# Odd mixer of a fused block kernel: a new order for the queues of ScalarE, VectorE and TensorE

## The chip, the cores and the metric

The kernel runs on one core of a Trainium2 chip. The metric is the device time of one execution in microseconds (us), the median of three runs. The core's engines each take their instructions from a queue of their own, in order, and wait for one another by semaphores: PE (TensorE, matmuls and transposes), DVE (VectorE), ACT (ScalarE), POOL (GpSimd) and SP, which issues the weight transfers. PEld is PE's weight load.

## What is computed

Two small transformer blocks in float32 on 256 tokens of width 1024, one after the other. The change is in the odd mixer, the Mamba-2 layer of the first block, cut here to what matters:

```
def odd_mixer(u, w_in, conv_w, conv_b, dt_bias, a_log, d_skip, out_norm_w, w_out):
    proj = (u @ w_in)
    z, xbc, dt = jnp.split(proj, [C_D_INNER, C_D_INNER + C_XBC], axis=-1)
    xbc = jax.nn.silu(causal_dwconv(xbc, conv_w) + conv_b)
    xs, b_in, c_in = jnp.split(xbc, ...)
    dt = jax.nn.softplus(dt + dt_bias)
    a = -jnp.exp(a_log) * dt
    y = ssd_chunked_scan(xs * dt[..., None], a, b_in, c_in) + d_skip[:, None] * xs
    y = y.reshape(bsz, seq, C_D_INNER) * jax.nn.silu(z)
    y = rmsnorm(y.reshape(bsz, seq, C_GROUPS, C_D_INNER // C_GROUPS), out_norm_w...)
    return (y.reshape(bsz, seq, C_D_INNER) @ w_out)
```

C_D_INNER is 2048, in four groups of 512 columns (8 heads of 64). The scan is over two blocks of 128 tokens here: what a block does within itself, and what the second gets from the state of the first.

## The kernel before

**Weights.** Every weight matrix comes from HBM in slots of 1 MB, each used as two granules of 128 x 1024. A float32 product is made of three matmuls on rounded parts, so each granule is split: ACT copies it to its high part (hi, L732, the copy is L741), DVE subtracts to get the low part (lo, L1373, L1379), PE multiplies high by high, low by high and high by low (L2182 to L2184, twelve matmuls to a granule). SPLITS = 4 granules can be held split: hi of granule g waits until PE has used granule g - 4 (gran_used), lo waits for hi, PE for lo. hi(k) and lo(k) in a queue stand for the next k granules.

**The odd mixer** (ACT L1065, DVE L1722, PE L2538) projects columns in the order OD_ORDER: B and C of the scan, dt, and then for the four groups in turn x and z. A projection is four granules into PSUM banks 0 and 1; out(k) on ACT (L1081) evicts it, and PE waits for that (proj_out) before the next projection writes these banks. B, C and the x of each group are turned to channels by PE (to_convolve, L2550), convolved (first_tap on ACT, L1091, convolve on DVE, L1732), put through Silu (conv_silu, L1100), and turned back (to_tokens, L2557; x_tokens, L1105, copies the result).

**The loop over g = 0, 1, 2** (ACT L1184, DVE L1831, PE L2637) does the scan of group g beside the projection of x of group g + 1 (beside_x) and of z of group g + 1 (beside_z; step k of them stands behind granule k). Its steps: c_times_b (PE L2564, copied by cb_copy, L1110); masked_decays (DVE L1751), rows (PE L2571, L2572) and exps (ACT L1123) make the decays of four heads, q = 0 to 3, in banks 4 and 5; segment (DVE L1768) multiplies them by c_times_b; weighted_x (DVE L1757 to L1759); state (PE L2578, copied by state_copy, L1115) and from_state (PE L2583) by way of bank 7; inside (PE L2595) into bank 6; skip (DVE L1773); gate (DVE L1783 to L1789) adds up and multiplies by z; squares, root, inverse_root, normed (ACT L1130, L1137, DVE L1794, ACT L1144) are the rmsnorm; turn_y (PE L2604), y_high (ACT L1151) and y_low (DVE L1801) bring the result to the two parts in which it goes into the last product. The work of group 3 stands behind the loop, beside the granules of w_out (down, L2233). All of this order is written out by hand, one list per engine.

## Time and profile before

| | us |
|---|---|
| median of 3 runs | 2990.28 (2987.95 to 2993.25) |
| the profiled execution | 2991.3 |
| its span | 2989.5 |
| PE, DVE, ACT busy in the span | 2772.0, 2100.8, 1682.2 |
| the loop, g = 0, 1, 2 (from the first matmul of its x projection to that of the next) | 47.4, 51.8, 44.9 to its last inside |
| from there to the last turn_last | 58.9 |

The page of the profile gives busy times by engine, the chain of work that ended last, and groups of instructions by source line. The trace gives single instructions with their start, their length and what ended the idle time before them, and sums over any stretch. PEclk, the clock that TensorE was granted, is a share of 2.4 GHz: 0.50 is 1.2 GHz. A row of windows gives the stretch and its length, then busy time and instructions of PE, PEld, DVE, ACT and POOL, PEclk, the DMA share and GB/s.

### The profile page before, as it was taken

The numbers are of one execution on the slowest core, as the hardware profiler recorded it, in microseconds if no ns is written. First come the engines' busy times: TensorE is split into PE (matmuls) and PEld (weight loads), VectorE is DVE, ScalarE is ACT, GpSimd is POOL, SyncE is SP. The second block draws the span as 40 slices with busy tenths as digits, with TensorE's granted clock in tenths as the row PEclk, the third lists the DMA queues.
The fourth block names the chain that finished last, engine by engine and source line by source line (L and its number), as shares of the span: only waits on it lengthen the run. The fifth ranks groups of instructions, "written<-read, shape, count | busy, mean of one in ns | idle before, by whom it ended". The sixth has DMA issues, their size and how long they took to land.

```text
span 2989.5 us, 35811 instructions
## 1 busy us (share of the span) xinstructions
PE 2772.0 (93%) x12921; PEld 2262.7 (76%) x12921; DVE 2100.8 (70%) x2339; ACT 1682.2 (56%) x2178; POOL 596.4 (20%) x321
## 2 busy tenths in 40 slices
PE   7999899999997799979778998799999999999997
PEld 6888778878976578868456887677878788787875
DVE  4556768778365565452458785588999888999897
ACT  4456454454275564442343443177777877778785
POOL 1000039999000000004007994000000000000000
PEclk9999999999899899989879998799999999999999
DMA  8545147778342245533017883189999999999994
GB/s 281 184 162 179 34 151 238 249 266 279 115 162 85 74 146 195 184 113 112 1 57 248 283 294 127 43 319 337 354 337 348 354 338 351 330 353 350 342 353 167
DMA packets 278012, 664.55 MB, mean 222 GB/s; under 512 B 12868, under 2 KB 21344, under 8 KB 277904
## 3 DMA queue, kind: packets, MB, share of 16 engines
q1 hardware_dynamic: 263344, 609.74, 57.7%
q0 software_dynamic: 14560, 53.36, 5.4%
q8 instruction: 70, 1.15, 0.2%
q14 instruction: 38, 0.31, 0.0%
HBM read 662.00 MB, written 1.05 MB: 222 GB/s over the span
## 4 chain that ended last, share of the span: by engine, by line
PE 79%; DVE 13%; ACT 5%; issue 2%; DMA 0%; DVEq 0%; ACTq 0%; SPq 0%
PE ps L2182 23%; PE ps L2184 23%; PE ps L2183 23%; DVE w_lo L1379 4%; ACT w_hi L741 2%; PE ps L2298 1%; PE ps L2852 1%; PE ps L2364 1%; PE ps L2766 1%; DVE xt L2054 1%; DVE small L1940 1%; PE ps L2728 1%; DVE xt L1732 1%; PE ps L2810 0%; DVE xn L1458 0%
## 5 line engine op out<-in xcount | busy, mean ns | idle before, releaser
L1379 DVE TENSOR_TENSOR w_lo<-w_raw,w_hi 128x1024 fp32r<-128x1024 f32 x1156 | 1534.9, 1352 | 522.5 <-ACT w_hi L741 496.3
L741 ACT ACTIVATE w_hi<-w_raw 128x1024 fp32r<-128x1024 f32 x1156 | 1210.3, 1058 | 835.0 <-PE ps L2184 834.2
L2182 PE MATMUL ps<-w_hi,act_hi 128*128 128x512 f32 (+1 forms) x3424 | 1353.4, 395 | 65.2 <-DVE w_lo L1379 33.5
L2184 PE MATMUL ps<-w_lo,act_hi 128*128 128x512 f32 (+1 forms) x3424 | 1327.9, 388 | 0.0
L2183 PE MATMUL ps<-w_hi,act_lo 128*128 128x512 f32 (+1 forms) x3424 | 1327.1, 388 | 0.0
L2182 PEld LDWEIGHTS ps<-w_hi,act_hi 128*128 128x128 f32 x3424 | 651.6, 190 | 213.9 <-DVE w_lo L1379 51.5
L2184 PEld LDWEIGHTS ps<-w_lo,act_hi 128*128 128x128 f32 x3424 | 650.9, 190 | 133.0
L2183 PEld LDWEIGHTS ps<-w_hi,act_lo 128*128 128x128 f32 x3424 | 652.1, 190 | 127.1 <-issue 3.5
L620 POOL TENSOR_TENSOR scr<-scr 128x1024 f32<-128x1024 f32 x98 | 287.3, 2932 | 8.2
L618 POOL TENSOR_SCALAR scr<-scr,small 128x1024 f32<-128x1024 f32 x98 | 194.7, 1987 | 6.4
L601 POOL DMA_DIRECT2D scr<-in_ada_w x48 | 36.8, 767 | 404.0 <-DVE h L1463 384.8
L872 ACT ACTIVATE act_hi<-ps 128x512 fp32r<-128x512 f32 (+1 forms) x87 | 62.7, 721 | 78.0 <-PE ps L2298 78.0
L1504 DVE TENSOR_TENSOR act_lo<-ps,act_hi 128x512 fp32r<-128x512 f32 (+1 forms) x87 | 73.9, 849 | 34.3 <-ACT act_hi L872 34.2
L2298 PEld LDWEIGHTS ps<-cst,hp 128*128 128x128 f32 x456 | 54.5, 140 | 24.5 <-DVE hp L1524 9.0
L674 POOL DMA_DIRECT2D scr<-in_ctx x1 | 0.8, 767 | 358.1 <-DVE h L1463 358.1
L2298 PE MATMUL ps<-cst,hp 128*128 128x128 f32 x456 | 64.2, 273 | 8.3 <-DVE hp L1524 6.9
L1528 DVE TENSOR_TENSOR hp<-sg,ps 128x512 f32<-128x512 f32 (+1 forms) x63 | 46.6, 740 | 33.1 <-PE ps L2184 33.1
L2273 PE MATMUL ps<-cst,xn 128*128 128x128 f32 x96 | 22.0, 424 | 42.9 <-DVE xn L1438 26.8
L1524 DVE SCALAR_TENSOR_TENSOR hp<-ps,rn,sg 128x512 f32<-128x512 f32 (+1 forms) x48 | 31.6, 700 | 36.1 <-PE ps L2184 36.1
L2273 PEld LDWEIGHTS ps<-cst,xn 128*128 128x128 f32 x96 | 19.7, 227 | 46.5 <-DVE xn L1438 21.2
L635 POOL TENSOR_TENSOR wbc<-xn,rope 128x512 f32<-128x512 f32 x2 | 2.7, 1364 | 239.8 <-ACT xn L1252 239.7
L1940 DVE TENSOR_REDUCE small<-ps 128x2 f32<-128x1024 f32 x16 | 19.6, 1224 | 35.2 <-PE ps L2766 35.2
(455 smaller groups left out, 1691.2 us busy)
## 6 DMA issues: line engine op xcount, KB each, us to landing
w_raw<-in_moe_w SPq DMA_DIRECT2D x336, 1024.0 KB, 6.9
scr<-in_ada_w POOLq DMA_DIRECT2D x48, 1024.0 KB, 5.9
w_raw<-in_ffn_w_gate SPq DMA_DIRECT2D x44, 1024.0 KB, 5.2
w_raw<-in_ffn_w_up SPq DMA_DIRECT2D x44, 1024.0 KB, 5.4
w_raw<-in_ffn_w_down SPq DMA_DIRECT2D x44, 1024.0 KB, 4.9
w_raw<-in_ff_w SPq DMA_DIRECT2D x42, 1024.0 KB, 5.9
w_raw<-in_odd_w_in SPq DMA_DIRECT2D x20, 1024.0 KB, 5.1
w_raw<-in_even_w_in SPq DMA_DIRECT2D x14, 1024.0 KB, 5.2
```

The costliest lines, as they stand in the source:

```text
L618: pool.tensor_scalar(product, w, x, 0.0, ALU.mult, ALU.add).then_inc(ada_mul, 1)
L620: pool.tensor_tensor(dst[:, cols], dst[:, cols], product, ALU.add).then_inc(ada_sum, 1)
L741: act.activation(w_hi[:, g % SPLITS, 0:c * width], w_raw[:, s % RING, o:o + c * width], ACT.Copy).then_inc(hi_done, 1)
L872: act.activation(act_hi[:, base:base + c, 0:tbs * P], src, ACT.Copy).then_inc(hhi_done, 1)
L1379: dve.tensor_tensor(w_lo[:, g % SPLITS, 0:c * width], w_raw[:, s % RING, o:o + c * width], w_hi[:, g % SPLITS, 0:c * width].bitcast(F32), ...
L1504: dve.tensor_tensor(act_lo[:, base:base + c, 0:tbs * P], src, act_hi[:, base:base + c, 0:tbs * P].bitcast(F32), ALU.subtract).then_inc(hlo ...
L1528: dve.tensor_tensor(view[0], view[1], ps[:, 6:6 + tbs, 0:width], ALU.mult).then_inc(hid_done, 1)
L1940: link(dve.tensor_reduce(m, ps[:, 2 * (u % 2):2 * (u % 2) + 2, :], AX_X, ALU.max))
L2182: pe.matmul(out_ap, hi, whi, start=start, stop=False)
L2183: pe.matmul(out_ap, lo, whi, start=False, stop=False)
L2184: return pe.matmul(out_ap, hi, wlo, start=False, stop=stop)
L2298: ins = pe.transpose(banks(6, tbs)[:, o:o + P], hp[:, tb * BANK + k * P:tb * BANK + k * P + P], ident)
```

## The change

Steps of the odd mixer's queues are put in another order on ACT, DVE and PE. Nothing is computed otherwise.

- hi and lo stand one granule at a time between the other steps, where they stood in twos; three granules of the next projection are split at the start of a turn of the loop, where it was four.
- out(5 + 2g) stands ahead of state_copy and of one more hi; out(6 + 2g) stands behind the first half of the Silu alone (conv_silu becomes two silu_half, and the second half moves into the next turn).
- gate(g, 1), squares(g, .) and root of a group move into the next turn. The product with the state that gate(g, 1) began with is a step of its own, from_before, with a semaphore of its own, og_or.
- On PE c_times_b stands behind granule 0 of x, both rows(0), rows(1) and to_tokens behind granule 1, state behind granule 3; both inside(g, 0), inside(g, 1) and to_convolve behind granule 0 of z. turn_y goes to banks 4 and 5, where it was 2 and 3.
- Behind the loop half_down does the first three granules of w_out for 128 tokens at a time, so that they can start before banks 2 and 3 are free.

On ACT, in turn 1 of the loop, from x_tokens (scr<-ps 128x2x512) to out (xn<-ps,rn). Before:

```order
L1105 ACTIVATE scr<-ps 128x2x512
L1110 ACTIVATE xt<-ps 128x256
L1144 ACTIVATE scr<-scr,rstd 128x512 x2
L1123 ACT_TABLE_LOAD
L1123 ACTIVATE hp<-ps,dtw 128x128 x4
L741 ACTIVATE w_hi<-w_raw 128x1024 x2
L1123 ACTIVATE hp<-ps,dtw 128x128 x4
L1115 ACTIVATE scr<-ps 128x512
L741 ACTIVATE w_hi<-w_raw 128x1024 x2
L1081 ACTIVATE xn<-ps,rn 128x512 x2
```

After (line numbers are up by 1 to 5; scr,ssq is squares, rt is root):

```order
L742 ACTIVATE w_hi<-w_raw 128x1024
L1115 ACTIVATE xt<-ps 128x256
L1135 ACTIVATE scr,ssq<-scr 128x512
L1142 ACT_TABLE_LOAD
L1142 ACTIVATE rt<-ssq,epsc 128x2
L742 ACTIVATE w_hi<-w_raw 128x1024
L1110 ACTIVATE scr<-ps 128x2x512
L1128 ACT_TABLE_LOAD
L1128 ACTIVATE hp<-ps,dtw 128x128 x8
L742 ACTIVATE w_hi<-w_raw 128x1024
L1149 ACTIVATE scr<-scr,rstd 128x512 x2
L1082 ACTIVATE xn<-ps,rn 128x512 x2
```

The eviction now stands behind two w_hi rather than four, and ahead of the copy of the state (scr<-ps 128x512); what was squares and root of the turn before stands here.

On DVE, from the end of turn 0 to the low part behind weighted_x (the three scr<-scr,dtw). Before:

```order
L1379 TENSOR_TENSOR w_lo<-w_raw,w_hi 128x1024
L1751 TENSOR_TENSOR sg<-cst,dtw 128x512 x2
L1794 RECIPROCAL rstd<-rt 128x2
L1379 TENSOR_TENSOR w_lo<-w_raw,w_hi 128x1024
L1757 TENSOR_TENSOR scr<-scr,dtw 128x512
L1758 TENSOR_TENSOR scr<-scr,dtw 128x512
L1759 TENSOR_TENSOR scr<-scr,dtw 128x512
L1379 TENSOR_TENSOR w_lo<-w_raw,w_hi 128x1024
```

After (line numbers are up by 19 to 21; the first three rows are what is left of gate(0, 1)):

```order
L1806 TENSOR_TENSOR scr<-scr,ps 128x512
L1809 TENSOR_TENSOR scr<-scr,xt 128x512
L1810 TENSOR_TENSOR scr<-scr 128x512
L1398 TENSOR_TENSOR w_lo<-w_raw,w_hi 128x1024
L1770 TENSOR_TENSOR sg<-cst,dtw 128x512 x2
L1398 TENSOR_TENSOR w_lo<-w_raw,w_hi 128x1024
L1815 RECIPROCAL rstd<-rt 128x2
L1398 TENSOR_TENSOR w_lo<-w_raw,w_hi 128x1024
L1776 TENSOR_TENSOR scr<-scr,dtw 128x512
L1777 TENSOR_TENSOR scr<-scr,dtw 128x512
L1778 TENSOR_TENSOR scr<-scr,dtw 128x512
L1398 TENSOR_TENSOR w_lo<-w_raw,w_hi 128x1024
```

Three w_lo stand between gate and weighted_x, one on each side of the decays (sg) and one behind the reciprocal, where one stood ahead of the decays and one behind the reciprocal.

On ACT, at the end of turn 1, from first_tap to the squares. Before:

```order
L1091 ACTIVATE xt<-ps,colv 128x256 x4
L741 ACTIVATE w_hi<-w_raw 128x1024
L1123 ACTIVATE hp<-ps,dtw 128x128 x4
L741 ACTIVATE w_hi<-w_raw 128x1024
L1100 ACT_TABLE_LOAD
L1100 ACTIVATE xt<-xt 128x512 x2
L741 ACTIVATE w_hi<-w_raw 128x1024 x2
L1081 ACTIVATE scr<-ps,rn 128x512 x2
L1130 ACTIVATE scr,ssq<-scr 128x512 x2
```

After:

```order
L1092 ACTIVATE xt<-ps,colv 128x256 x4
L742 ACTIVATE w_hi<-w_raw 128x1024
L1128 ACTIVATE hp<-ps,dtw 128x128 x4
L742 ACTIVATE w_hi<-w_raw 128x1024
L1128 ACTIVATE hp<-ps,dtw 128x128 x4
L1100 ACT_TABLE_LOAD
L1100 ACTIVATE xt<-xt 128x512
L1082 ACTIVATE scr<-ps,rn 128x512 x2
L1100 ACTIVATE xt<-xt 128x512
```

Between the last exps and the eviction of z (scr<-ps,rn) one half of the Silu is left; two w_hi and the other half are gone from there.

The diff, cut to what the working speaks of (ACT, DVE, PE):

```diff
-                hi(2)
+                hi(1)
                 first_tap(2)
                 hi(2)
+                silu_half(2, 0)
                 out(4)
-                conv_silu(2)
-                act.wait_ge(sv_in, n(sv_in))
-                act.activation(dtw[:, T_ECUM, :], dtw[:, T_CUM, :], ACT.Exp)
-                act.activation(dtw[:, T_EDEC, :], dtw[:, T_REST, :], ACT.Exp).then_inc(sv_out, 1)

                 for g in range(3):
+                    silu_half(2 + g, 1)
+                    hi(1)
+                    if g:
+                        squares(g - 1, 0)
+                    hi(1)
+                    cb_copy()
+                    if g:
+                        squares(g - 1, 1)
+                        root(2 * g - 2, 2)
+                    else:
+                        act.wait_ge(sv_in, n(sv_in))
+                        act.activation(dtw[:, T_ECUM, :], dtw[:, T_CUM, :], ACT.Exp)
+                        act.activation(dtw[:, T_EDEC, :], dtw[:, T_REST, :], ACT.Exp).then_inc(sv_out, 1)
+                    hi(1)
                     x_tokens(g)
-                    cb_copy()
+                    exps(g, 0, 4)
+                    exps(g, 1, 5)
+                    hi(1)
                     if g:
                         normed(g - 1, 0)
                         normed(g - 1, 1)
-                    exps(g, 0, 4)
-                    hi(2)
-                    exps(g, 1, 5)
+                    out(5 + 2 * g)
+                    hi(1)
                     state_copy()
-                    hi(2)
-                    out(5 + 2 * g)
                     if g:
-                        y_high(g - 1, 0, 2)
-                        y_high(g - 1, 1, 3)
-                    exps(g, 2, 4)
+                        y_high(g - 1, 0, 4)
+                        y_high(g - 1, 1, 5)
+                    hi(1)
                     first_tap(3 + g)
                     hi(1)
+                    exps(g, 2, 4)
+                    hi(1)
                     exps(g, 3, 5)
-                    hi(1)
-                    conv_silu(3 + g)
-                    hi(2)
+                    silu_half(3 + g, 0)
                     out(6 + 2 * g)
-                    squares(g, 0)
-                    squares(g, 1)
-                    root(2 * g, 2)
-
+
...
+                def from_before(g):
+
+                    dve.wait_ge(og_off, n(og_off))
+                    dve.tensor_tensor(eight(o_off), eight(ps[:, 7, :]), bc(of(T_ECUM, 1, g), C_DIM), ALU.mult).then_inc(og_or, 1)
+
...
+                        dve.wait_ge(og_or, g + 1)
                         link(dve.tensor_tensor(x, x, o_off, ALU.add))
...
                 for g in range(3):
+                    if g:
+                        gate(g - 1, 1)
+                    lo(1)
                     masked_decays(g, 0)
                     masked_decays(g, 1)
+                    lo(1)
+                    if g:
+                        inverse_root(2 * g - 2, 2)
+                    lo(1)
                     if g == 0:
                         dve.wait_ge(sv_out, n(sv_out))
-                    else:
-                        inverse_root(2 * g - 2, 2)
-                    lo(1)
                     weighted_x(g)
                     lo(1)
                     segment(0)
+                    segment(1)
                     masked_decays(g, 2)
-                    lo(1)
-                    segment(1)
                     masked_decays(g, 3)
                     skip(g, 0)
                     lo(1)
+                    if g:
+                        y_low(g - 1, 0, 4)
+                        y_low(g - 1, 1, 5)
                     gate(g, 0)
-                    if g:
-                        y_low(g - 1, 0, 2)
-                        y_low(g - 1, 1, 3)
-                    segment(2)
                     lo(1)
                     convolve(3 + g, 0)
-                    segment(3)
                     lo(1)
-                    convolve(3 + g, 1)
+                    from_before(g)
+                    segment(2)
                     skip(g, 1)
                     lo(1)
-                    gate(g, 1)
-                    lo(1)
-
+                    segment(3)
+                    convolve(3 + g, 1)
+
+                gate(2, 1)
+                lo(1)
                 masked_decays(3, 0)
                 masked_decays(3, 1)
+                segment(0)
+                segment(1)
+                masked_decays(3, 2)
+                masked_decays(3, 3)
+                weighted_x(3)
                 inverse_root(4, 2)
...
+                def half_down(chunks, tb, skip=0):
+
+                    for k, chunk in enumerate(chunks):
+                        g = gp[0] + skip + k
+                        pe.wait_ge(lo_done, g + 1)
+                        for nh in range(2):
+                            ins = three(ps[:, 2 * tb + nh, :], chunk, slice(tb * P, tb * P + P), g, nh * BANK, BANK,
+                                        skip + k == 0, False)
+                        if tb:
+                            ins.then_inc(gran_used, 1)
...
                     def beside_x(k):
                         if k == 0:
+                            if g:
+                                pe.wait_ge(og_or, g)
+                            c_times_b(g)
+                        if k == 1:
+                            if g:
+                                pe.wait_ge(og_e, 4 * g)
+                            rows(0, 4)
+                            rows(1, 5)
                             pe.wait_ge(cv_act, CV + 2 * (3 + g))
                             to_tokens(2 + g, 2)
-                        if k == 1:
-                            rows(0, 4)
+                        if k == 3:
+                            state(g)
                             if g:
-                                pe.wait_ge(og_yz, 2 * g)
-                            c_times_b(g)
-                        if k == 2:
-                            rows(1, 5)
-                            state(g)
-                        if k == 3:
-                            inside(g, 0)
-                            if g:
+                                pe.wait_ge(og_e, 4 * g + 2)
                                 pe.wait_ge(og_n, 2 * g)
-                                pe.wait_ge(o_tc, 2 + g)
-                                turn_y(g - 1, 0, 2)
-                                turn_y(g - 1, 1, 3)
+                                turn_y(g - 1, 0, 4)
+                                turn_y(g - 1, 1, 5)
...
                     def beside_z(k):
                         if k == 0:
+                            inside(g, 0)
                             inside(g, 1)
+                            pe.wait_ge(o_tc, 2 + g)
+                            to_convolve(3 + g)
+                        if k == 1:
                             pe.wait_ge(og_e, 4 * g + 1)
+                            if g:
+                                pe.wait_ge(og_lo, 2 * g - 1)
                             rows(2, 4)
-                        if k == 1:
+                            from_state(g)
+                        if k == 2:
                             pe.wait_ge(og_e, 4 * g + 2)
-                            rows(3, 5)
-                            from_state(g)
-                            pe.wait_ge(o_tc, 2 + g)
                             if g:
                                 pe.wait_ge(og_lo, 2 * g)
-                            to_convolve(3 + g)
-                        if k == 2:
+                            rows(3, 5)
+                        if k == 3:
                             inside(g, 2)
-                        if k == 3:
                             inside(g, 3)
...
+                pe.wait_ge(og_or, 3)
+                c_times_b(3)
+                pe.wait_ge(og_e, 12)
+                rows(0, 4)
+                rows(1, 5)
+                pe.wait_ge(proj_out, 8 + 11)
+                pe.wait_ge(og_lo, 4)
+                half_down((o_slot(0), o_slot(1)), 0)
                 pe.wait_ge(cv_act, CV + 12)
                 to_tokens(5, 2)
-                pe.wait_ge(og_yz, 6)
...
+                half_down((o_slot(2),), 0, 2)
                 pe.wait_ge(o_tc, 5)
-                down((o_slot(0),), True)
-                pe.wait_ge(og_n, 6)
-                turn_y(2, 0, 5)
+                half_down((o_slot(0), o_slot(1), o_slot(2)), 1)
+                gp[0] += 3
                 state(3)
-                down((o_slot(1),))
+                down((o_slot(3),))
                 inside(3, 0)
...
                 inside(3, 1)
                 pe.wait_ge(og_e, 14)
+                pe.wait_ge(og_n, 6)
+                turn_y(2, 0, 4)
+                turn_y(2, 1, 5)
+                down((o_slot(4),))
+                from_state(3)
+                down((o_slot(5),))
+                pe.wait_ge(og_lo, 6)
                 rows(2, 4)
-                from_state(3)
-                down((o_slot(4), o_slot(5)))
+                rows(3, 5)
+                down((o_slot(6),))
                 inside(3, 2)
```

## Rows read from the trace of the kernel before

**Rows 1.** The page: the chain that ended last, shares by engine.

```profile
PE 79%; DVE 13%; ACT 5%; issue 2%; DMA 0%; DVEq 0%; ACTq 0%; SPq 0%
```

**Rows 2.** Windows: turns 1 and 2, the tail behind the loop, turn 0.

```profile
937.50:989.30 51.80, 39.92 (x172) 30.24 (x172) 28.26 (x45) 27.70 (x52) 0.00 (x0) 0.86 0.23 82
989.30:1034.20 44.90, 39.32 (x172) 29.82 (x172) 22.75 (x35) 24.00 (x46) 0.00 (x0) 0.91 0.20 71
1034.20:1093.10 58.90, 49.67 (x224) 38.52 (x224) 37.30 (x55) 36.55 (x64) 0.00 (x0) 0.91 0.35 112
890.10:937.50 47.40, 37.21 (x164) 28.39 (x164) 26.57 (x45) 23.64 (x44) 0.00 (x0) 0.90 0.27 89
```

**Rows 3.** Waits in turn 1: who for whom, us in total, times, longest.

```profile
DVE w_lo L1379 <- ACT w_hi L741: 19.2, 4, 11.3
...
PE ps L2182 <- ACT scr L1081: 6.3, 1, 6.3
...
PE ps L2578 <- DVE scr L1759: 4.4, 1, 4.4
```

**Rows 4.** Windows behind two waits of PE in turn 2.

```profile
989.00:994.50 5.50, 5.18 (x13) 4.02 (x14) 4.60 (x8) 3.18 (x7) 0.00 (x0) 0.53 0.16 26
...
1008.00:1011.00 3.00, 2.93 (x5) 1.71 (x6) 2.35 (x4) 0.82 (x2) 0.00 (x0) 0.50 0.16 35
```

**Rows 5.** Timeline of ACT, turn 1: start, length, instruction [idle before it <-releaser].

```profile
943.98 1.03 ACT L1105 ACTIVATE scr<-ps 128x1024 f32<-128x1024 f32 x1 [2.21 <-PE ps L2557]
...
948.53 1.32 ACT L1144 ACTIVATE scr<-scr,rstd 128x512 f32<-128x512 f32 x2
949.87 1.28 ACT L1123 ACT_TABLE_LOAD   x1
951.17 1.14 ACT L1123 ACTIVATE hp<-ps,dtw 128x128 f32<-128x128 f32 x4
...
985.60 0.63 ACT L1100 ACTIVATE xt<-xt 128x512 f32<-128x512 f32 x1 [3.70 <-DVE xt L1732]
986.13 1.99 ACT L741 ACTIVATE w_hi<-w_raw 128x1024 fp32r<-128x1024 f32 x2
988.02 1.24 ACT L1081 ACTIVATE scr<-ps,rn 128x512 f32<-128x512 f32 x2
```

**Rows 6.** Timeline of DVE, turn 1.

```profile
953.29 1.23 DVE L1379 TENSOR_TENSOR w_lo<-w_raw,w_hi 128x1024 fp32r<-128x1024 f32 x1 [11.33 <-ACT w_hi L741]
...
955.76 0.68 DVE L1759 TENSOR_TENSOR scr<-scr,dtw 128x512 f32<-128x512 f32 x1
...
982.89 2.67 DVE L1732 SCALAR_TENSOR_TENSOR xt<-ps,colv,xt 128x255 f32<-128x255 f32 x6
...
989.06 0.69 DVE L1786 TENSOR_TENSOR scr<-scr,ps 128x512 f32<-128x512 f32 x1
```

**Rows 7.** Timeline of PE, turn 1, at the full clock.

```profile
971.92 0.39 PE L2571 MATMUL ps<-negr,identr 128*128 128x512 f32 x1
...
973.01 1.02 PE L2583 MATMUL ps<-scr 128*128 128x512 f32 x2
973.86 1.04 PE L2550 MATMUL ps<-cst,xn 128*128 128x128 f32 x8
974.66 0.47 PE L2182 MATMUL ps<-w_hi,act_hi 128*128 128x512 f32 x1
...
977.50 1.00 PE L2595 MATMUL ps<-scr,hp 128*128 128x64 f32 x8
978.31 0.48 PE L2182 MATMUL ps<-w_hi,act_hi 128*128 128x512 f32 x1
```

**Rows 8.** Timeline of PE: waits ahead of turn 0 and behind turn 2.

```profile
890.08 0.79 PE L2182 MATMUL ps<-w_hi,act_hi 128*128 128x512 f32 x1 [4.01 <-ACT scr L1081]
...
1037.75 1.22 PE L2557 MATMUL ps<-cst,xt 128*128 128x128 f32 x8 [3.28 <-ACT xt L1100]
1042.73 1.22 PE L2564 MATMUL ps<-scr 128*128 128x128 f32 x4 [3.76 <-DVE scr L1789]
```

82 lines of the change are left out of this document (35 added, 47 removed).

## The prediction

> **What bounds the kernel now.** Look first at the chain that ended last: 79% of it lies on PE [rows 1]. So nearly everywhere only PE's own work counts, and another engine matters where PE waits. The next view, busy time by window, shows that the odd mixer is such a place [rows 2]: PE is busy 39.9 us of the 51.8 us of turn 1, while DVE is busy 28.3 and ACT 27.7. No engine is full, so the turn is as long as a chain that runs from engine to engine. From the first matmul of turn 0 to the last turn_last the odd mixer takes 47.4 + 51.8 + 44.9 + 58.9 = 203.0 us [rows 2].
>
> The waits of turn 1 say where PE stands still [rows 3]: 6.3 us for an eviction on ACT, 4.4 us for weighted_x on DVE. The timeline of ACT shows the first: behind the second half of the convolution come Silu at 985.60, two w_hi from 986.13, and only at 988.02 the eviction of z, though PE has stood since 983 [rows 3, 5]. The timeline of DVE shows the second: it stands 11.3 us at a low part (953.29) whose high part is queued on ACT behind x_tokens and the exps; weighted_x, which needs no weights, sits behind it until 955.76 + 0.7, and state on PE waits for it [rows 6]. The third cost follows from the two: behind each long wait the granted clock is 0.50 to 0.53 for 5.5 us and 3.0 us [rows 4], that is the lower level of 1.2 GHz.
>
> **What PE must do in a turn.** In rows at the full clock one granule takes 977.50 - 974.66 = 2.84 us, a call of rows 973.01 - 971.92 = 1.09, from_state 0.85 (state the same), eight transposes 974.66 - 973.86 = 0.80, inside 978.31 - 977.50 = 0.81 [rows 7]. A turn has 8 granules (22.7), 4 rows (4.4), 4 inside (3.2), state and from_state (1.7), three sets of eight transposes (2.4), c_times_b (four short ones, 0.4): 34.8 us. Turn 1 takes 51.8, so 17 us are waits and low clock.
>
> **The new order, walked through for one turn.** Zero is the first matmul of x. Durations besides those above, as the distance to the next instruction: w_hi 0.95, an eviction 1.2, x_tokens 1.0, both normed 1.3, a table load 1.28, an exps 1.0, Silu 0.6 [rows 5]; w_lo 1.14, a convolution half 2.6, the three steps of gate 2.1 [rows 6].
>
> First half. PE: granule 0 to 2.8, c_times_b, granule 1 to 6.1, two rows to 8.3, to_tokens to 9.1, granules 2 and 3 to 14.8, state to 15.6, turn_y. ACT: Silu half, w_hi, squares, w_hi (free from 2.8), cb_copy, squares, root with its load, w_hi (free from 6.1) until 7.3; then it waits for to_tokens: x_tokens 9.1 to 10.1, load 11.4, exps twice 13.5, w_hi 14.4, normed 15.7, eviction of x 16.9. PE's turn_y waits for normed until 15.7 and ends at 16.5, so PE loses 0.1 ahead of it and 0.4 to the eviction, with a semaphore or two 0.7 in all. DVE: gate 2.2, w_lo 3.3, decays 4.6 (wanted at 6.1), two w_lo to 8.5, weighted_x 10.1 to 12.1, wanted by state at 14.8. The wait of 4.4 is gone, with 2.7 us to spare, and the low parts of x are ready 8 us early.
>
> Second half, from 17. PE: granule 19.8, two inside 21.4, to_convolve 22.2, granule 25.1, rows 26.2, from_state 27.0, granule 29.9, rows 31.0, granule 33.8, two inside 35.4. ACT: copies and y_high until 20, w_hi, first_tap 22.2 to 24, w_hi 26, exps 27.3, w_hi 30.9, exps 32.0, load 33.3, Silu half 33.9, eviction of z 35.1. PE's two inside (1.6 us) cover it. DVE: y_low 21.6, gate 23, w_lo and convolution half 26.8, w_lo, from_before and segment 29.3, skip, w_lo 32, segment 32.7 (wanted at 34.6), the other half 35.3, and gate in the next turn. The wait of 6.3 is gone: its cover is inside, which is 1.6 long against 1.2. Without a long wait the clock stays up.
>
> So a turn takes 34.8 + 0.7 = 35.5 us. Turn 0 has no turn_y (-0.8) but starts behind a wait as now, at the lower level for one granule (+2.3: 13 matmuls took 5.5 us there [rows 4], so twelve 5.1 against 2.8): 37.0. **Ahead of turn 0** one w_hi fewer stands before the eviction that PE waits 4.0 us for [rows 8]; one half of the Silu is moved ahead of it (0.6). I take 1.0 us, bounds 0 and 4.
>
> **The tail.** Before, PE waits 3.3 us for the Silu and 3.8 us for gate [rows 8], with smaller waits behind. After, its work is 12 granules in whole or halves (34.1), 4 rows (4.4), 4 inside (3.2), two products with the state (1.7), transposes 0.8 + 0.8 + 0.8, c_times_b 0.4: 46.2. The new order puts both rows ahead of the first granule, and they wait for DVE: gate(2, 1) 2.1, a w_lo 1.1, the first decays 0.6 stand before them, and c_times_b covers 0.4: a new wait of 3.5 us. Whether the clock falls after it is open: it did behind 6.3 and 4.4 us [rows 4], and I charge 2 us (bounds 0 and 4). Walked on as above, each later step has its input: 46.2 + 5.5 = 51.7.
>
> **Edits at no cost.** from_before adds no instruction, only its own place. Two stores of decays in banks 4 and 5 rather than one at a time, and turn_y there rather than in 2 and 3, add waits of PE (og_e, og_lo) that the walk finds met 1 us or more early. half_down does the same matmuls. SP's weight loads follow the low parts; the DMA engines are busy 0.20 to 0.35 of these stretches [rows 2] and would be at 0.3 to 0.4. POOL is idle here and not touched.
>
> **The sum.** After: 37.0 + 35.5 + 35.5 + 51.7 = 159.7, against 203.0: 43.3, and 1.0 ahead of turn 0: 44.3 us less. What follows the odd mixer is shifted. The profiled execution took 2991.3, 1.0 above the median, so 2947.0 for it and **2946 us** as a median.
>
> A rule that speaks against this: ACT changes its function set three times a turn in both orders, and one of these loads now stands between to_tokens and the eviction of x. In the rows a load starts 0.02 us behind the last normed and the exps starts 1.30 us after the load started [rows 5]. The Trainium skill, in "ScalarE: Activation LUTs", section "What ACT_TABLE_LOAD costs", gives the same 1283 ns for the load and adds a drain of about 1380 ns for each switch. The trace does not show that drain here, and the measurement decides.
>
> **The rivals.**
> - *The queues trail.* ACT has 7.8 us of steps between to_tokens and the end of the eviction of x, PE 7.4 us: any step that ACT starts late comes out on PE, and DVE carries 28 us in 35. For it: PE near full, DVE and ACT near 80%, tied at each granule. Against: the spare times above. Turns of 39 to 43 and a tail a little longer: 10 to 25 us of the gain are lost, 2953 to 2972.
> - *Each load also drains*, by the rule above. An extra 1.4 us per load would lie on PE's path once a turn and once in the tail: 5.6, so 2952. Against: the two rows of the load.
> - *The wait only moves.* PE would wait as long at the evictions, because the high parts ahead of them wait for PE. Against: in the walk ACT waits for PE to free a high part only right behind granules, never with an eviction due. 2984 to 2996.
> - *Starved for low parts (slower).* Only three granules are split at the start of a turn, and the fourth low part sits behind gate, which waits for the last inside of the turn before. It decides once DVE comes to it more than 8 us late, since granule 3 starts at 12.0. Then each granule waits for a w_hi and a w_lo in a row: 2.1 us times 24, and the clock falls to the lower level, 2.3 us times 24; less the 44: about 3050.
>
> **How the numbers follow.** Forecast 0.65, with its own range 2936 to 2953: 2936 is every wait and low clock above at nothing (0.7 x 3 + 2.3 + 5.5, and the bounds). Trailing queues 0.22, drains 0.03, a moved wait 0.05, starved 0.05. The range of 2935 to 2967 holds the first and the third and most of the second, 0.8 in all. A measurement of this kernel can tell about 0.2%, 6 us, from no change. Faster by more: 0.65 + 0.22 + 0.03 + 0.02 of the moved wait; the same: 0.02; slower: 0.05 and 0.01.
>
> **What would show it.** In the profile after: turns of 35 to 36 us; the two waits of 6.3 and 4.4 gone from PE's list, PEclk near 1.00 in turns 1 and 2; DVE's waits for w_hi no longer than 2 to 3 us; a PE wait of about 3.5 us for the decays at the start of the tail. I am wrong if ACT's Silu waits long for the convolution at a turn's start, if PE waits at state, or if low parts are late for granule 3.

## The result

| kernel | median us | runs | lowest, highest | ratio to before, 95% interval |
|---|---|---|---|---|
| before | 2989.11 | 4 | 2987.43, 2993.25 | |
| changed | 2950.3 | 4 | 2948.82, 2951.35 | 0.9875 [0.9861, 0.9889] |

The change saves 38.8 us by the medians, 1.3%; the ratio in the table, which is not the quotient of the two medians, says 1.25%, with an interval of 1.1 to 1.4%. The profiled execution of the changed kernel took 2948.8 us (span 2946.9), that of the kernel before 2991.3 (span 2989.5): 42.5 us between the two profiles. The median before is 1.2 us lower than the one the prediction started from, because a fourth run has come in.

The page of the changed kernel, the chain that ended last (before: 79% on PE [rows 1]):

```profile
PE 81%; DVE 12%; ACT 4%; issue 2%; DMA 0%; DVEq 0%; ACTq 0%; SPq 0%
```

Windows of the changed kernel, in the same columns as [rows 2] (window, its length, busy time and count of PE, weight loads, DVE, ACT, POOL, then the granted clock, DMA share, GB/s): turn 0, turn 1, turn 2, the tail to the end of the last turn_last.

```profile
892.88:929.06 36.18, 35.68 (x164) 27.80 (x165) 26.60 (x44) 22.81 (x41) 0.00 (x0) 0.95 0.43 143
929.06:964.73 35.67, 35.15 (x175) 27.54 (x174) 28.19 (x45) 27.77 (x51) 0.00 (x0) 1.00 0.34 119
964.73:1000.42 35.69, 35.16 (x174) 27.54 (x174) 28.19 (x45) 27.78 (x51) 0.00 (x0) 1.00 0.35 118
1000.42:1052.41 51.99, 48.36 (x223) 37.64 (x222) 31.74 (x46) 32.70 (x60) 0.00 (x0) 0.93 0.34 106
```

Turn 1 went from 51.8 to 35.7 us, turn 2 from 44.9 to 35.7, turn 0 from 47.4 to 36.2, the tail from 58.9 to 52.0. The four sum to 159.5, against 203.0. In turn 1 DVE and ACT are busy 28 us, as before, but in a turn that is 16 us shorter. The clock is at 1.00 (2.4 GHz) through turns 1 and 2, where it was 0.86 and 0.91.

Waits in turn 1 (who for whom: us in total, times, longest), against [rows 3]. The list has no line of PE for an eviction or for weighted_x any more, and DVE's 19.2 us behind high parts are 4.5:

```profile
ACT w_hi L742 <- PE ps L2208: 4.8, 4, 2.5
DVE w_lo L1398 <- ACT w_hi L742: 4.5, 3, 2.4
```

In the first line ACT waits for PE to free the slot of a high part; before the change that line stood at 2.0 us. It is the healthy direction, since PE is the engine that is to be full.

The timeline of PE in the changed kernel shows the waits that are left: one ahead of turn 0, one of half a microsecond in turn 0 and in turns 1 and 2 (turn 1's is shown), one at the start of the tail.

```profile
892.88 0.50 PE L2206 MATMUL ps<-w_hi,act_hi 128*128 128x512 f32 x1 [3.59 <-ACT scr L1082]
...
910.55 0.50 PE L2206 MATMUL ps<-w_hi,act_hi 128*128 128x512 f32 x1 [0.50 <-ACT xn L1082]
...
945.16 1.07 PE L2628 MATMUL ps<-cst,scr 128*128 128x128 f32 x8 [0.52 <-ACT scr L1149]
...
1004.72 0.76 PE L2595 MATMUL ps<-negr,identr 128*128 128x512 f32 x1 [3.63 <-DVE sg L1770]
```

Windows of PE alone (busy, clock, DMA share, GB/s) around the wait of the tail: up to its end, the 5.5 us behind it, and the time after.

```profile
1000.40:1004.70 4.30, 0.69 (x6) 0.78 0.00 0
1004.70:1010.20 5.50, 5.49 (x10) 0.55 0.61 191
1010.20:1023.80 13.60, 13.60 (x72) 1.00 0.11 29
```

**A measure that the clock elsewhere does not blur.** For comparing the experiments the span is split at two instructions which all kernels have: the first transposes of four in the odd mixer, to_tokens(0) (873.24 before, 876.47 after), and the last turn_last (1092.48 before, 1052.02 after). Between the two lies all that the change touches; it is called the stretch below. It is 219.2 us before and 175.6 after: 43.7 less. PE executes the same instructions in the part ahead of it in every kernel here, and so it does in the part behind.

### The profile page after: what moved, and what is told of

The parts are those of the page before. It is cut to its first block, busy times and chain, and to the rows that moved or that the text cites. A ratio compares the mean times of both kernels' runs of the same rounds, so it can differ in the third digit from the quotient of the medians.

```text
span 2946.9 us, 35814 instructions
## 1 busy us (share of the span) xinstructions
PE 2758.8 (94%) x12921; PEld 2256.2 (77%) x12921; DVE 2085.5 (71%) x2339; ACT 1680.7 (57%) x2177; POOL 590.6 (20%) x321
## 4 chain that ended last, share of the span: by engine, by line
PE 81%; DVE 12%; ACT 4%; issue 2%; DMA 0%; DVEq 0%; ACTq 0%; SPq 0%
PE ps L2206 24%; PE ps L2208 24%; PE ps L2207 24%; DVE w_lo L1398 4%; ACT w_hi L742 2%; PE ps L2322 1%; PE ps L2388 1%; PE ps L2892 1%; PE ps L2806 1%; DVE xt L2078 1%; DVE small L1964 1%; PE ps L2768 1%; PE ps L2596 0%; DVE xn L1477 0%; PE ps L2850 0%
## 5 line engine op out<-in xcount | busy, mean ns | idle before, releaser
L1964 DVE TENSOR_REDUCE small<-ps 128x2 f32<-128x1024 f32 x16 | 19.6, 1224 | 35.9 <-PE ps L2806 35.9
```

What stands on the lines that cost most here:

```text
L1964: link(dve.tensor_reduce(m, ps[:, 2 * (u % 2):2 * (u % 2) + 2, :], AX_X, ALU.max))
```

## The experiments

Each of the twelve kernels was profiled and timed, two of them twice. The twelve share one kernel before, which was timed again with each set, so each ratio is to runs of its own set. All profiles, split in the three parts (us):

| kernel | part ahead | stretch | part behind | ratio to before, 95% interval |
|---|---|---|---|---|
| before | 873.2 | 219.2 | 1897.0 | |
| changed | 876.5 | 175.6 | 1894.9 | 0.9875 [0.9861, 0.9889] |
| changed_again | 874.0 | 175.6 | 1894.8 | 0.9872 [0.9856, 0.9887] |
| loop_alone | 873.9 | 176.5 | 1893.7 | 0.9871 [0.9854, 0.9887] |
| loop_alone_again | 873.0 | 176.3 | 1894.3 | 0.9863 [0.9846, 0.9880] |
| z_evicted_late | 873.8 | 186.0 | 1897.7 | 0.9890 [0.9874, 0.9907] |
| high_parts_late | 868.3 | 188.6 | 1895.3 | 0.9897 [0.9879, 0.9914] |
| decays_first | 876.7 | 170.0 | 1893.4 | 0.9849 [0.9832, 0.9865] |
| head | 868.6 | 173.0 | 1897.3 | 0.9840 [0.9825, 0.9855] |
| head_and_decays | 874.6 | 168.0 | 1896.9 | 0.9830 [0.9816, 0.9843] |
| head_decays_too | 876.4 | 165.7 | 1892.1 | 0.9818 [0.9805, 0.9832] |
| eviction_alone | 874.8 | 211.7 | 1894.4 | 0.9975 [0.9962, 0.9989] |
| high_part_early_alone | 872.8 | 204.5 | 1893.1 | 0.9953 [0.9936, 0.9969] |
| both_places | 879.3 | 198.1 | 1897.9 | 0.9915 [0.9899, 0.9931] |

The theory of the prediction: two waits of a turn set its length, one for the eviction of z that stands behind high parts on ACT, one for weighted_x that stands behind a late high part on DVE; the rest is steps that are off PE's path once moved. Rival one: only one of the two counts, the other is covered. Rival two: the tail's gain comes from the lead of the queues, not from the tail's own order.

### Undoing one thing in the changed kernel

**z_evicted_late**

```diff
                 for g in range(3):
-                    silu_half(2 + g, 1)
-                    hi(1)
+                    if not g:
+                        silu_half(2, 1)
+                        hi(1)
...
                     silu_half(3 + g, 0)
+                    silu_half(3 + g, 1)
+                    hi(1)
                     out(6 + 2 * g)
```

> The changed kernel with one thing put back: ScalarE's second half of the Silu of Z and a w_hi (about 3.1 us) stand ahead of the eviction of Z again, on which the next turn's matmuls wait. If the eviction's place is what took the 6.3 us wait away, each turn has a wait of 2 to 3.5 us on TensorE for the eviction, turns of 38 to 39 us, and if the clock falls behind it 39 to 40: 8 to 13 us more in all (2958 to 2963). If the order of the high parts carries the gain instead, the wait stays under 1 us and the time within 2 us of 2950.

Measured: the stretch is 10.5 us longer (186.0). PE's wait for the eviction is back in turns 0 and 1, 2.83 us each, and the clock falls behind it:

```profile
929.38 0.79 PE L2207 MATMUL ps<-w_hi,act_hi 128*128 128x512 f32 x1 [2.83 <-ACT scr L1082]
```

```profile
929.30:933.30 4.00, 3.92 (x9) 3.14 (x10) 1.83 (x3) 0.64 (x3) 0.00 (x0) 0.50 0.54 161
```

Nine matmuls in 4.0 us, where at full clock 17 or 18 fit (below): here a wait of 2.8 costs 5 us in all. The stretch lies in the expected 8 to 13 us, though by two waits and not three: at the end of turn 2 the eviction is covered by the wait of 3.6 us that the tail has anyway, and turn 1 is 41.3 us, more than the 39 to 40 expected. The medians say less. 2955.1 is 4.8 above the changed kernel, under the expected range, and the intervals overlap; beside loop_alone, which was timed in the same set (2947.2), it is 7.9, where the stretches differ by 9.5.

**high_parts_late**

```diff
-                    hi(1)
                     cb_copy()
...
-                    hi(1)
                     x_tokens(g)
                     exps(g, 0, 4)
+                    hi(2)
                     exps(g, 1, 5)
```

> The changed kernel with the other thing put back: the two high parts of Z stand as a pair behind x_tokens and the first exps on ScalarE, as before the change. If VectorE's wait for a high part (11.3 us before the change, 2.4 in the changed kernel) is what held back weighted x, VectorE waits 4 to 6 us for w_hi in each turn, TensorE's state waits 2 to 4 us for weighted x, and each turn is 38 to 41 us: 8 to 15 us more (2958 to 2965). If only the eviction counts, the turns stay at 35.5 to 36.5 and the time within 2 us of 2950.

Measured: the stretch is 13.1 us longer (188.6). In turn 1 the wait list of this kernel has DVE at 9.0 us for one high part, and PE at 3.4 us for weighted_x:

```profile
DVE w_lo L1397 <- ACT w_hi L742: 10.4, 2, 9.0
ACT w_hi L742 <- PE ps L2207: 6.9, 3, 3.1
...
PE ps L2601 <- DVE scr L1777: 3.4, 1, 3.4
```

```profile
940.50:944.50 4.00, 3.99 (x11) 2.77 (x12) 4.00 (x6) 3.43 (x7) 0.00 (x0) 0.50 0.56 228
```

This is the chain that the prediction read out of the kernel before, made again by two moved lines: high part late, low part late, weighted_x late, state late, clock down (the window above starts at state). DVE's wait is 9.0, not the 4 to 6 that was expected, because x_tokens, behind which the high parts stand, waits 3.19 us for to_tokens on PE itself; the table load and the exps follow, and the w_hi comes only at 935.00, without a wait of its own:

```profile
931.65 1.03 ACT L1110 ACTIVATE scr<-ps 128x1024 f32<-128x1024 f32 x1 [3.19 <-PE ps L2580]
...
935.00 2.02 ACT L742 ACTIVATE w_hi<-w_raw 128x1024 fp32r<-128x1024 f32 x2
```

Here too the medians say less than the stretch: 2955.6 is 5.3 above the changed kernel and 8.4 above loop_alone of the same set. The rival in which only the eviction counts is out, and z_evicted_late rules out its opposite; both rest on the stretch, in which the waits themselves can be seen.

**loop_alone**, and the same kernel again as **loop_alone_again**

The loop is the changed kernel's; the steps of ACT, DVE and PE behind it are those of before (the product of from_before(3) stands right ahead of gate(3, 1), whose first step it was; half_down is gone). The start of it on DVE:

```diff
                 masked_decays(3, 1)
+                inverse_root(4, 2)
+                weighted_x(3)
                 segment(0)
-                segment(1)
                 masked_decays(3, 2)
+                y_low(2, 0, 5)
+                lo(2)
+                segment(1)
                 masked_decays(3, 3)
-                weighted_x(3)
-                inverse_root(4, 2)
                 skip(3, 0)
-                lo(4)
-                gate(3, 0)
```

> The loop of the changed kernel with the tail of the kernel before: granule 3's exps, weighted x and segments stand behind the loop again, and segment work is not spread over turn 2. If the saving comes from two separate places as the prediction's sum has it (loop and tail), the three turns stay at 36 to 37, 35.5 and 35.5 us, and the tail behind turn 2 (to the last granule's turn_last) is 58 to 59 us again instead of 51.6: 7 us longer than the changed kernel, about 2957. If the tail is short only because the loop leaves the queues further ahead, the tail stays at 52 to 53 and the time within 1 us of the changed kernel.

> New loop and old tail once more, beside the changed kernel on the same chip. The trace of the first run has 176.5 us for the stretch from the first transposed group to the last turn, the changed kernel 175.5: so 0 to 2 us slower than the changed kernel if the trace decides. If the tail's rearrangement were worth the 7 us that the first expectation of this kernel gave it, 7 us slower.

Measured: the three turns are 36.3, 35.7 and 35.9 us, as in the changed kernel, and the old tail is not 58 to 59 but 52.6 (to the end of its last turn_last):

```profile
998.20:1050.80 52.60, 48.30 (x222) 37.62 (x221) 32.05 (x46) 34.26 (x61) 0.00 (x0) 0.97 0.36 116
```

The stretch is 176.5 and 176.3, 0.9 and 0.8 longer than the changed kernel's. So the expectation that the tail's new order is worth 7 us fell, and the rival stands. Rows of PE in the old tail behind the new loop say why:

```profile
998.94 1.09 PE L2582 MATMUL ps<-cst,xt 128*128 128x128 f32 x8 [0.74 <-ACT xt L1100]
...
1000.51 0.71 PE L2589 MATMUL ps<-scr 128*128 128x128 f32 x4 [0.47 <-DVE scr L1809]
...
1002.24 0.50 PE L2596 MATMUL ps<-negr,identr 128*128 128x512 f32 x1 [1.02 <-DVE sg L1769]
...
1036.39 1.10 PE L2620 MATMUL ps<-scr,hp 128*128 128x64 f32 x8 [1.67 <-DVE hp L1786]
```

The waits for the Silu and for gate, 3.28 and 3.76 us before [rows 8], are 0.74 and 0.47 with the tail's own steps in the old order: in the new loop ACT and DVE are less behind when the loop ends. What the new tail does is trade these small waits (with one of 0.38 they sum to 4.3, and behind the one of 1.67 the clock is 0.65 and 0.69 in the two profiles) for one of 3.63 and 2 us of lower clock. The medians of the pair timed on one chip are 2949.3 (changed_again) and 2948.6: no difference that can be measured.

**changed_again**

No edit.

> The changed kernel itself, on the chip and beside the runs on which the next three are timed. By the first timing it is 38.8 us faster than before. If what differs between profiles outside the odd mixer is the clock's chance dips, its stretch from the first transposed group to the last turn is 175.5 us again to 0.2 us, while the whole moves by up to 4 us.

Measured: stretch 175.56, against 175.55 in the first profile; ratio 0.9872; 39.9 us between the medians. The part ahead is 2.5 us shorter than in the first profile, with the same instructions.

### Doing one thing in the kernel before

**eviction_alone**

```diff
-                    conv_silu(3 + g)
-                    hi(2)
+                    silu_half(3 + g, 0)
                     out(6 + 2 * g)
+                    silu_half(3 + g, 1)
+                    hi(2)
```

> The kernel before with one part of the change alone: the eviction of Z stands right behind the first half of the Silu and ahead of the other half and both high parts. The 6.3 us wait at the end of a turn should fall under 1 us. If the two waits of a turn are separate, turns fall from 45 to 52 us to 39 to 44: about 20 us less in all (2970). If the queues of ScalarE and VectorE trail as a whole, the wait comes back in the next turn at c_times_b, rows or state, and the saving is 3 to 10 us (2980 to 2986).

**high_part_early_alone**

```diff
                 for g in range(3):
+                    hi(1)
                     x_tokens(g)
                     cb_copy()
...
                     exps(g, 0, 4)
-                    hi(2)
+                    hi(1)
                     exps(g, 1, 5)
```

> The kernel before with the other part alone: one high part ahead of x_tokens and one behind the first exps instead of a pair there. VectorE's wait for w_hi (up to 11.3 us) falls, and weighted x comes earlier: the wait of state for it (4.4 us) falls to 0 to 2, while the wait for the eviction (6.3 us) stays or grows by what the others lose. 5 to 15 us less in all (2975 to 2985) if the two are separate; within 3 us of the kernel before if the eviction alone sets the turn.

Measured: 7.6 and 14.8 us off the stretch; by the medians 7.9 and 13.9. Earlier high parts alone bring more than the eviction alone. For eviction_alone 20 us were expected if the two waits are separate; that fell, and the other branch came (3 to 10 us, the wait comes back). In eviction_alone PE's wait of 6.3 us is gone, but part of it comes back at once as a wait for the decays, which stand behind gate on DVE; the wait for weighted_x is untouched. PE's waits between 930 and 955 us:

```profile
PE ps L2584 <- DVE scr L1765: 4.4, 1, 4.4
PE ps L2577 <- DVE sg L1757: 2.9, 1, 2.9
```

Behind this wait of 2.9 us for the decays the clock held at 1.00, both times that the kernel has it (the windows are in the last section).

In high_part_early_alone it is the other way round: the wait for weighted_x is gone from PE's list, and the one for the eviction stays at 6.3 in both turns.

**both_places**: the two edits together.

> The kernel before with both single parts at once: the eviction of Z between the two half Silus, and one high part ahead of x_tokens instead of two behind the first exps. Alone they took 7.6 and 14.8 us off the stretch from the first transposed group to the last turn. If they are independent, 22 us less than before, 2964 to 2966. If each only exposes the wait that the other removes, more than the sum: 30 to 38 us, and the rest of the change (gate, norm and y moved into the next turn) is worth little. If gate and c_times_b's wait sets the end of a turn in both, less than the sum, 15 to 20 us, and the moved steps carry the rest.

Measured: the stretch is 21.1 us shorter than before (198.1), by the medians 23.1. That is the sum of the two within 1.3 us, so they add. The three profiles differ in dips of the clock as well, of about 1.6 us each (an estimate from eleven matmuls rather than eighteen in 4 us): one in high_part_early_alone (behind a wait of 1.46 us), two in both_places (behind its waits of 2.87). With these taken out it is 24.3 against 7.6 + 16.4 = 24.0, the same finding. It is half of the 43.7. What PE still waits for between 942 and 985 us, the better part of a turn:

```profile
PE ps L2578 <- DVE sg L1758: 2.9, 1, 2.9
PE ps L2189 <- ACT xn L1081: 0.6, 1, 0.6
PE ps L2602 <- DVE hp L1775: 0.6, 1, 0.6
```

The other half (198.1 to the 176.4 of loop_alone, 21.7 us) belongs to what else the new loop moves: gate, squares and root into the next turn, the decays ahead of what waits, one granule's parts at a time, other banks. The first of these lines is the wait for the decays, which stand behind gate in its old place. Part of the 21.7 is the lead into the tail: PE still waits 3.29 and 3.02 us at the tail's start in both_places, 0.74 and 0.47 in loop_alone. Which of the moved steps is worth how much was not tried apart.

### Better than both kernels

**decays_first**

```diff
-                gate(2, 1)
-                lo(1)
                 masked_decays(3, 0)
                 masked_decays(3, 1)
+                gate(2, 1)
+                lo(1)
```

> The changed kernel with VectorE's two masked decays of granule 3 ahead of a gate and a low part, which nothing in the tail's start waits for. The wait of 3.6 us that TensorE has for the decays at the tail's start should be 0.3 to 0.8, and the granules behind it should not run at half clock (another 2 us): tail 46.5 to 47.5 instead of 51.6, the whole about 2945. If the clock does not come back with the wait, the gain is 3 us. If the gate is then late for normed and the last from_before, the wait turns up further down the tail and the time stays at 2949 to 2950.

Measured: the wait is 0.27, the clock stays at 1.00, and the tail is 45.9 us to the start of its last turn_last (the window reaches to its end). The stretch is 5.6 shorter, a little more than expected (the tail 51.6 less 45.9); the wait gives 3.4 of it and what is left, 2.2, goes to the clock. The median is 2942.0, where about 2945 was expected.

```profile
1001.70 0.47 PE L2595 MATMUL ps<-negr,identr 128*128 128x512 f32 x1 [0.27 <-DVE sg L1770]
```

```profile
1000.77:1047.03 46.26, 45.99 (x223) 36.53 (x222) 31.63 (x46) 32.62 (x60) 0.00 (x0) 1.00 0.39 119
```

**head**

```diff
                 act.activation(dtw[:, T_E, :], dtw[:, T_ABS, :], ACT.Exp, scale=-1.0).then_inc(act_link, 1)
+                act.activation(work[:, 0:32], m_alog, ACT.Exp)
                 act.wait_ge(act_link, n(act_link))
-                act.activation(dtw[:, T_LN, :], dtw[:, T_E, :], ACT.Ln, bias=1.0)
-                act.activation(work[:, 0:32], m_alog, ACT.Exp).then_inc(sv_out, 1)
+                act.activation(dtw[:, T_LN, :], dtw[:, T_E, :], ACT.Ln, bias=1.0).then_inc(sv_out, 1)
...
                 first_tap(2)
-                hi(2)
-                silu_half(2, 0)
+                hi(1)
                 out(4)
+                hi(1)
+                silu_half(2, 0)
```

> The changed kernel with two edits ahead of turn 0: ScalarE's Exp of the decay rates stands beside the other Exp, so that one table load of three is not needed, and the eviction that turn 0 waits for stands ahead of one high part and a half Silu. TensorE's wait ahead of turn 0 (3.6 us in the changed kernel) should be 0.5 to 1.0 us, and the clock should not fall to half for the first 4 us of turn 0: 3 to 5 us less, 2945 to 2947. If the wait was for the eviction but another step (a low part of VectorE) is next in line just behind it, 1 to 2 us less. If the head's wait is covered by something later, no change.

**head_and_decays**: both.

> Both edits, at the head and at the tail's start. If the two waits are independent stretches of one path, the gains add: 8 to 10 us less than the changed kernel, 2940 to 2942, with neither wait above 1 us. If the clock's dips only move to other short waits, 5 us less, 2945.

Measured in head: the wait ahead of turn 0 is 0.96 instead of 3.59 and the clock stays at 1.00, but 8 us later a new wait for the decays of turn 0 appears, so the stretch gets only 2.6 shorter, under the 3 to 5 expected (the median moved more, see the last section):

```profile
882.37 0.50 PE L2207 MATMUL ps<-w_hi,act_hi 128*128 128x512 f32 x1 [0.96 <-ACT scr L1082]
...
890.65 0.50 PE L2596 MATMUL ps<-negr,identr 128*128 128x512 f32 x1 [2.06 <-DVE sg L1771]
```

With both edits the stretch is 7.5 shorter, against 2.6 + 5.6: they add within 0.7. That is less than the 8 to 10 expected, and the wait of 2.06 in turn 0 is still there, above the 1 us that the expectation allowed; the median, 2933.9, is lower than the 2940 to 2942 expected.

**head_decays_too**: both, and in turn 0 the decays ahead of the low part.

```diff
-                    lo(1)
+                    if g:
+                        lo(1)
                     masked_decays(g, 0)
                     masked_decays(g, 1)
-                    lo(1)
+                    lo(1 if g else 2)
```

> The changed kernel with the two edits at head and tail, and a third: in turn 0 VectorE's masked decays stand ahead of a low part whose high part comes late, since the trace of the two edits shows a new wait of 2.1 us for the decays in turn 0. That wait should fall to 0 to 0.7 us; with it 2 to 4 us less than both edits without it, the stretch from the first transposed group to the last turn 164 to 166 us instead of 168.0. If the low part that is now later is what turn 0 needs next, the wait moves to w_lo and the stretch stays at 168.

Measured: the new wait is gone, the stretch is 165.7. Its windows (three turns and the tail) have the clock at 1.00 throughout, and PE idles 0.3 to 0.5 us in each:

```profile
890.13:924.85 34.72, 34.22 (x165) 26.66 (x165) 28.43 (x46) 23.91 (x43) 0.00 (x0) 1.00 0.47 152
924.85:960.57 35.72, 35.19 (x175) 27.53 (x173) 28.18 (x45) 27.80 (x51) 0.00 (x0) 1.00 0.35 118
...
996.25:1042.50 46.25, 45.99 (x223) 36.53 (x222) 31.61 (x46) 32.63 (x60) 0.00 (x0) 1.00 0.38 119
```

Its median is 2936.8 us, 12.5 below the changed kernel on the same chip (2949.3), ratio 0.9818 [0.9805, 0.9832] against 0.9872 [0.9856, 0.9887]. Its stretch and its ratio are the lowest of all kernels here. Next to head_and_decays (0.9830, median 2933.9 in another set) only the stretch tells them apart, by 2.3 us; the intervals overlap.

## Why the prediction was right, point by point

- **The time.** 2946 was forecast, 2950.3 measured, in the range and in the likeliest case's own range (2936 to 2953).
- **The bound.** "The turn is as long as a chain that runs from engine to engine": shown from both sides. Either link alone, put back, makes turn 1 5.6 and 5.7 us longer (41.3 and 41.4 against 35.7); either alone, mended, shortens the stretch by 7.6 and 14.8.
- **The walk of a turn.** 35.5 forecast, 35.67 and 35.69 measured. PE's work is 35.15 rather than 34.8, and its stall 0.52 rather than 0.7, so two small errors cancel in part. The stall is all ahead of turn_y, where 0.1 was forecast; the 0.4 at the eviction of x is nothing in turns 1 and 2. DVE's longest wait for a high part is 1.9 in turn 0 and 2.4 in turns 1 and 2 (no longer than 2 to 3 forecast).
- **Turn 0.** 37.0 forecast, 36.2 measured. The lower level was charged for twelve matmuls at 2.3 us; they took 4.44 us (clock 0.62 on average, not 0.5), which is 1.6 more than 2.84.
- **Ahead of turn 0.** 1.0 us forecast, 0.4 measured (16.84 from to_tokens(0) to turn 0 before, 16.41 after). The step at fault is its own arithmetic: one w_hi fewer (0.95) and half a Silu more (0.6) are 0.35, and the prediction took 1.0 without saying why. Rows of ACT in the changed kernel show the half Silu, with its table load, right ahead of the eviction (before the change a table load stood there too, of the eviction's own, so that this one adds nothing):

```profile
887.72 2.01 ACT L742 ACTIVATE w_hi<-w_raw 128x1024 fp32r<-128x1024 f32 x2
889.75 1.28 ACT L1100 ACT_TABLE_LOAD   x1
891.04 0.63 ACT L1100 ACTIVATE xt<-xt 128x512 f32<-128x512 f32 x1
891.58 1.25 ACT L1082 ACTIVATE scr<-ps,rn 128x512 f32<-128x512 f32 x2
```

- **The tail.** 51.7 forecast, 51.6 measured to the start of the last turn_last; the new wait 3.5 forecast, 3.63 measured, with the clock's 2 us behind it (2.2 by decays_first). The size was right. What the prediction did not see is that most of the tail's gain needed none of the tail's edits: with the old tail behind the new loop the stretch is 0.9 longer, no more.
- **The sum.** 44.3 forecast for the odd mixer with its head; the stretch has 43.7. The saving between the medians is 38.8 and 39.9, some 4 to 5 us less, and this part of the forecast is unaccounted for. The prediction took the rest of the kernel to be "shifted" and no more, and the profiles do not show otherwise: outside the stretch the first profile of the changed kernel is 1.1 us longer than that of the kernel before (3.2 longer ahead, 2.1 shorter behind), the second is 1.5 us shorter (0.7 longer ahead, 2.3 shorter behind), and the whole of it is 45.2 us shorter than the profile before. That 2946 came so near owes 1.2 us to the base, which was 2990.28 and is 2989.11 now: by the saving the forecast is 5.5 us too high, by the time 4.3 too low.
- **The rivals.** Queues that trail: turns of 39 to 43 did not come, though the load is as it said (DVE and ACT busy 28 of 35.7 us). A wait that only moves: none did in turns 1 and 2 (the 3.63 of the tail was in the forecast). Starved low parts: no PE wait for w_lo in any turn. The drain of each table load: in the rows below ACT's load starts at 939.38 and the exps 1.30 us after it, as before the change, and the turn has no 1.4 us too many. The Trainium skill ("ScalarE: Activation LUTs", section "What ACT_TABLE_LOAD costs") adds a drain for each switch, and no row here shows one; the measurement decides.

```profile
939.38 1.28 ACT L1128 ACT_TABLE_LOAD   x1
940.68 2.17 ACT L1128 ACTIVATE hp<-ps,dtw 128x128 f32<-128x128 f32 x8
```

## What to carry to other kernels

Where three engines are each busy for less than 80% of a loop and none is full, read for each wait of the critical engine what is queued ahead of its releaser, and ask whether that needs to be there; here two such places gave 21 us together, about the sum of what each gave alone. Before crediting an edit at the end of a pipeline, run the new loop with the old end: the lead that the queues bring out of the loop may already have paid for it. And price a wait of some 3 us on TensorE at up to 5: in the stretch the clock fell behind every wait of 3.0 us or more, which cost about 2 us on top, and behind four of six of 2.8 to 2.9.

## What the runs showed of the hardware

**Behind a wait of one and the same length the clock falls in some executions and holds in others.** In the stage that follows the odd mixer, PE waits 1.51 us for a low part in every profile. The instructions around it are the same in all. In nine of the fourteen profiles the granted clock stays at 1.00 behind it; in five (changed, changed_again, z_evicted_late, eviction_alone, both_places) it is 0.57 to 0.61 for the next 4 us. The windows of PE that begin at the end of this wait, of the kernel before, then of the changed kernel, then of loop_alone:

```profile
1111.20:1115.20 4.00, 4.00 (x18) 1.00 0.95 315
```

```profile
1070.74:1074.74 4.00, 4.00 (x11) 0.57 0.99 314
```

```profile
1069.12:1073.12 4.00, 4.00 (x18) 1.00 0.94 317
```

Eighteen matmuls or eleven in the same 4 us. From the last turn_last to the next wait of 1.57 us it is 41.2 us in the changed kernel and 39.6 in loop_alone: such a dip costs 1.6 us. Behind that second wait the clock dips in seven profiles too (0.71 in the changed kernel) and holds in seven (1.00 before). All waits of PE of 0.9 us or more from the start of the stretch to the end of this stage's second wait, with the granted clock of the next 4 us:

| wait, us | granted clock behind it |
|---|---|
| 0.96 to 1.02 | 1.00 in all five |
| 1.46 | 1.00 in three profiles, 0.64 in high_part_early_alone |
| 1.51 | 1.00 in nine, 0.57 to 0.61 in five |
| 1.57 | 1.00 in seven, 0.66 to 0.73 in seven |
| 1.67 | 1.00 in the four with the loop of before, 0.65 and 0.69 in the two of loop_alone |
| 1.84 to 2.06 | 1.00 in all five |
| 2.83 to 2.88 | 1.00 twice (eviction_alone), 0.50 twice (z_evicted_late), 0.57 and 0.63 (both_places) |
| 3.01 and more | 0.50 to 0.61 in all |

The widest case is one and the same wait for the decays, first in eviction_alone, then in both_places, each with the window of PE behind it:

```profile
942.77 0.50 PE L2577 MATMUL ps<-negr,identr 128*128 128x512 f32 x1 [2.87 <-DVE sg L1757]
```

```profile
942.77:946.77 4.00, 4.00 (x18) 1.00 0.77 262
```

```profile
945.16 0.50 PE L2578 MATMUL ps<-negr,identr 128*128 128x512 f32 x1 [2.87 <-DVE sg L1758]
```

```profile
945.16:949.16 4.00, 4.00 (x11) 0.57 0.70 262
```

Both profiles of the changed kernel have the two dips behind the stretch, and the profile before has neither, which could be some 3 us of what the forecast missed. Two things speak against it: the part behind is 2 us shorter than before in both profiles in spite of the dips, and loop_alone has neither dip in its two profiles while its median is that of the changed kernel. So the cause of the 4 us stays open.

**Equal code takes unequal time.** The part ahead of the stretch, the same instructions in all fourteen profiles, took from 868.3 (high_parts_late) to 879.3 us (both_places). These two rows are the same four transposes:

```profile
868.30 0.60 PE L2580 MATMUL ps<-cst,scr 128*128 128x128 f32 x4
```

```profile
879.26 0.60 PE L2564 MATMUL ps<-cst,scr 128*128 128x128 f32 x4
```

Two edits of 3 us each can thus not be told apart by the span of a profile, while the stretch repeated within 0.2 us in the two kernels that were profiled twice (175.55 and 175.56; 176.5 and 176.3). It is not free of chance either: the dip behind the wait of 1.46 us lies in it, and in high_part_early_alone it makes the way to PE's next wait 1.6 us longer than before.

**The medians scatter about the stretch.** Against the kernel before of its own set, a median saves from 4.9 us less to 2.0 us more than the stretch, over thirteen timings: the changed kernel 38.8 and 39.9 for 43.7, decays_first 45.0 for 49.3, loop_alone 39.8 and 40.6 for 42.8 and 42.9, head 48.0 for 46.3, both_places 23.1 for 21.1. The forecast's missing 4 us are the low end of this scatter. It bears on a second riddle: head is timed 10.5 us faster than the changed kernel by the ratios (0.9840 against 0.9875 of 2989, intervals that do not meet), but its stretch is only 2.6 shorter; 4.9 of the difference is what the changed kernel's median falls short of its stretch. No run tells whether the scatter is chance or has a cause outside the stretch.
